# Hybrid encoder block with product-key experts: the last four value tiles by result block, four weight buffers, and norm_final's vector ahead of the root

## What is computed

```python
def peer_ffn(x, ...):           # g: softmax weights of the picked experts, u, v: their rows
    a = gelu(einsum('td,thkd->thk', xb, u))
    return einsum('thk,thkd->td', g * a, expert_v[idx])

h = h + peer_ffn(rmsnorm(h, norm_ffn), ...)
return rmsnorm(h, norm_final)   # y * rsqrt(mean(y*y) + 1e-6) * norm_final
```

## Time and profile before

| | |
|---|---|
| median of 3 runs | 1021.51 us (1021.49 to 1021.79) |
| the profiled execution | 1021.52 us, its span 1019.7 us |
| TensorE matmul busy | 1009.3 us, 99% of the span |
| VectorE, ScalarE, GpSimd busy | 847.5, 599.5, 81.1 us |
| granted TensorE clock, mean | 0.998 |

### The profile page before, as it was taken

The page is one execution under the profiler, slowest core; times in us unless marked ns, Lnnn a source line. Parts: engine busy times, 40 slices in busy tenths (PEclk is TensorE's granted clock), DMA queues, the critical chain, the costliest instruction groups (busy, mean ns, idle before and its releaser), DMA issues.

```text
span 1019.7 us, 20585 instructions
## 1 busy us (share of the span) xinstructions
PE 1009.3 (99%) x6978; PEld 929.4 (91%) x6978; DVE 847.5 (83%) x1686; ACT 599.5 (59%) x1109; POOL 81.1 (8%) x38
## 2 busy tenths in 40 slices
PE   9999999999999999999999999999999999999997
PEld 8989899999999999999999999988888888888885
DVE  7886868679999999999999999777777777777775
ACT  6456544644545468888888888555554544445453
POOL 0000000067780000000000000000000000000000
PEclk9999999999999999999999999999999999999999
DMA  8534334645577766666566665886676676666761
GB/s 332 189 132 143 126 139 168 201 170 207 172 234 230 237 220 209 208 209 206 199 218 208 209 206 198 274 319 232 232 233 233 232 239 235 234 231 238 234 232 67
DMA packets 86597, 215.00 MB, mean 211 GB/s; under 512 B 9600, under 2 KB 42752, under 8 KB 86016
## 3 DMA queue, kind: packets, MB, share of 16 engines
q1 hardware_dynamic: 86240, 213.53, 61.9%
q10 hardware_dynamic: 288, 0.53, 0.1%
HBM read 195.15 MB, written 18.87 MB: 210 GB/s over the span
## 4 chain that ended last, share of the span: by engine, by line
PE 95%; DVE 3%; ACT 1%; issue 1%; DMA 0%; DVEq 0%; ACTq 0%
PE pO L1087 34%; PE pO L1336 18%; PE pTT L1361 18%; PE pM L1361 17%; PE pSS L1310 1%; PE pTT L1310 1%; PE pSS L1157 1%; PE pM L1194 1%; PE pSS L1279 1%; DVE wlos L666 1%; DVE gates L689 0%; DMA raw<-in_stream 0%; PE pTT L1176 0%; DVE biasm L828 0%; PE pM L1188 0%
## 5 line engine op out<-in xcount | busy, mean ns | idle before, releaser
L456 ACT ACTIVATE whis<-raw 128x1024 fp32r<-128x1024 f32 x328 | 344.6, 1051 | 46.6 <-PE pO L1087 34.6
L666 DVE TENSOR_TENSOR wlos<-raw,whis 128x1024 fp32r<-128x1024 f32 x170 | 206.3, 1217 | 21.2 <-ACT whis L456 20.8
L1087 PE MATMUL pO<-xhi,whis 128*128 128x256 f32 x760 | 214.9, 283 | 0.7 <-DVE wlos L666 0.7
L1087 PE MATMUL pO<-xlo,whis 128*128 128x256 f32 x760 | 212.3, 279 | 0.0
L1087 PE MATMUL pO<-xhi,wlos 128*128 128x256 f32 x760 | 212.1, 279 | 0.0
L1003 DVE TENSOR_TENSOR wlos<-raw,whis 128x1024 fp32r<-128x1024 f32 x125 | 153.2, 1226 | 64.1 <-ACT whis L456 64.0
L616 ACT ACTIVATE ghi<-wfull 128x256 fp32r<-128x256 f32 x128 | 53.5, 418 | 171.8 <-PE pM L1361 171.8
L1087 PEld LDWEIGHTS pO<-xhi,whis 128*128 128x128 f32 x760 | 142.7, 188 | 2.0 <-DVE wlos L666 1.6
L1336 PE MATMUL pO<-xlo,whis 128*128 128x256 f32 x512 | 143.4, 280 | 0.0
L1336 PE MATMUL pO<-xhi,wlos 128*128 128x256 f32 x512 | 143.0, 279 | 0.0
L1336 PE MATMUL pO<-xhi,whis 128*128 128x256 f32 x512 | 143.0, 279 | 0.0
(11 more groups left out here) (215 smaller groups left out, 1882.7 us busy)
## 6 DMA issues: line engine op xcount, KB each, us to landing
raw<-in_stream SPq DMA_DIRECT2D x200, 512.0 KB, 3.6
raw<-in_vrows SPq DMA_DIRECT2D x128, 512.0 KB, 3.5
a_scratch<-ast SPq DMA_DIRECT2D x128, 128.0 KB, 1.8
aring<-a_scratch SPq DMA_DIRECT2D x128, 128.0 KB, 3.2
biasm<-in_bias SPq DMA_DIRECT2D x1, 2048.0 KB, 9.6
keysT<-in_keys SPq DMA_DIRECT2D x1, 1024.0 KB, 8.0
h_scratch<-h1tok SPq DMA_DIRECT2D x1, 1024.0 KB, 6.4
htok<-h_scratch SPq DMA_DIRECT2D x1, 1024.0 KB, 8.6
```

Of the source, the lines that this page charges most:

```text
L456: act.activation(whi[s], raw[s][:], ACT.Copy).then_inc(hi_ready, 1)
L666: dve.tensor_tensor(wlo[t % RING], raw[t % RING][:], whi[t % RING].bitcast(F32), ALU.subtract).then_inc(lo_ready, 1)
L1087: last = pe.matmul(dst, st, mv, start=(c == 0 and q == 0), stop=(c == len(terms) - 1 and q == 2))
```

## The change

The last four value tiles are taken out of the tile order. TensorE goes over five pieces of the result, and for each over the four tiles 124 to 127 and their three terms, twelve matmuls. The pieces are three blocks of 512 columns and, for the last 512 columns of the second token block, two of 256. The last two pieces are summed in the banks pO, free by then, and what tiles 0 to 123 have summed in acc[1][1] is added to htok beforehand. For that the high and low weights ghi and glo get four buffers each instead of two, and ghi waits for the tile four back. The loop's first tile moves from 4 to 3.

In the tail the first token block is treated as before. In the second, each piece is multiplied with norm_final before the root is known (gained), by an operation of its own, and afterwards only with the reciprocal: columns 0 to 767 on VectorE, stored by SP, and columns 768 to 1023 on ScalarE, stored by ScalarE's queue. The sum of the first two pieces is scaled by 1/1024 on VectorE and enters the root as its bias. Squares are written to a PSUM bank in place of the SBUF tile fsq.

```diff
+PIECES = ((0, 0, 512), (0, 512, 1024), (1, 0, 512), (1, 512, 768), (1, 768, 1024))
+BY_DVE = 768
...
+        ends = [pT[0], pT[1], pM[0][:], pO[0][:, 0:T], pO[1][:, 0:T]]
...
-                    act.wait_ge(tile_done, i + (T_V - 1))
-                act.activation(ghi[s % 2][:], wfull[s % 2][:], ACT.Copy).then_inc(ghi_ready, 1)
+                    act.wait_ge(tile_done, i + (T_V - RING + 1))
+                act.activation(ghi[s % RING][:], wfull[s % 2][:], ACT.Copy).then_inc(ghi_ready, 1)
...
+            piece_sum(0)
+            piece_sum(1)
+            act.wait_ge(fin_ms, 1)
+            act.activation(fin[:, 6:7], fin[:, 5:6], ACT.Sqrt, scale=1.0 / D).then_inc(fin_root, 1)
+            piece_sum(2)
+            piece_sum(3)
+            piece_sum(4)
+            act.wait_ge(fin_sum, 5)
+            act.wait_ge(fin_ms, 2)
+            act.activation(fin[:, 9:10], fin[:, 4:5], ACT.Sqrt, scale=1.0 / D, bias=fin[:, 8:9]).then_inc(fin_root, 1)
+            act.wait_ge(fin_inverse, 2)
+            act.wait_ge(gained_out, 3)
+            act.activation(htok[:, 1, BY_DVE:D], htok[:, 1, BY_DVE:D], ACT.Copy, scale=fin[:, 10:11]).then_inc(act_rows, 1)
+            act.wait_ge(act_rows, 1)
+            act.dma_start(out[:, 1, BY_DVE:D], htok[:, 1, BY_DVE:D]).then_inc(out_stored, 16)
...
-                dve.tensor_tensor(glo[s % 2][:], wfull[s % 2][:], ghi[s % 2][:].bitcast(F32), ALU.subtract).then_inc(glo_ready, 1)
+                dve.tensor_tensor(glo[s % RING][:], wfull[s % 2][:], ghi[s % RING][:].bitcast(F32), ALU.subtract).then_inc(glo_ready, 1)
...
+            def gained(j):
+
+                b, lo, hi = PIECES[j]
+                dve.wait_ge(fin_sum, j + 1)
+                dve.tensor_tensor(htok[:, b, lo:hi], htok[:, b, lo:hi], gf[:, lo:hi], ALU.mult).then_inc(gained_out, 1)
...
+            dve.wait_ge(tile_done, T_V + NE_TILES - RING)
+            link(dve.tensor_tensor(htok[:, 1, 512:D], acc[1][1], htok[:, 1, 512:D], ALU.add))
             residual(0)
             residual(1)
+            dve.wait_ge(fin_sum, 2)
+            dve.scalar_tensor_tensor(fin[:, 5:6], fin[:, 0:1], D * EPS, fin[:, 1:2], ALU.add, ALU.add).then_inc(fin_ms, 1)
+            dve.wait_ge(fin_root, 1)
+            dve.reciprocal(fin[:, 7:8], fin[:, 6:7]).then_inc(fin_inverse, 1)
+            dve.wait_ge(fin_inverse, 1)
+            rows_out(0)
             residual(2)
-            whole_sum(0)
+            rows_out(1)
             residual(3)
...
+            gained(2)
+            gained(3)
+            dve.wait_ge(fin_sum, 4)
+            link(dve.scalar_tensor_tensor(fin[:, 11:12], fin[:, 2:3], D * EPS, fin[:, 3:4], ALU.add, ALU.add))
+            dve.tensor_scalar(fin[:, 8:9], fin[:, 11:12], 1.0 / D, None, ALU.mult).then_inc(fin_ms, 1)
+            residual(4)
+            gained(4)
+            dve.wait_ge(fin_root, 2)
+            dve.reciprocal(fin[:, 10:11], fin[:, 9:10]).then_inc(fin_inverse, 1)
+            dve.wait_ge(fin_inverse, 2)
+            dve.wait_ge(gained_out, 3)
+            dve.tensor_scalar(htok[:, 1, 0:BY_DVE], htok[:, 1, 0:BY_DVE], fin[:, 10:11], None, ALU.mult).then_inc(out_ready, 1)
...
+            def v_last_tiles():
+
+                for j, (b, lo, hi) in enumerate(PIECES):
+                    last = None
+                    for s in range(RING):
+                        if (b, lo) == (0, 0):
+                            v_wait(NE_TILES - RING + s)
+                        for n, (st, mv) in v_terms(s, b):
+                            last = pe.matmul(ends[j], st, mv[:, lo:hi], start=hi - lo < 512 and s == 0 and n == 0, stop=s == RING - 1 and n == 2)
+                    last.then_inc(acc_done, 1)
```

More of the change, by code:

```diff
@@ L222, in build @@
         G = sbs(top, "G", [P, T, NK])
-        fin = sbs(top, "fin", [P, 10])
+        fin = sbs(top, "fin", [P, 12])
         iota = sbs(top, "iota", [P, P])[:]
@@ L235, in build @@
             gf = sbs(vphase, "gf", [P, D])
-            fsq = sbs(vphase, "fsq", [P, D])
-            glo = [sbs(vphase, f"glo{s}", [P, T], F32R) for s in range(2)]
+            ghi_more = [sbs(vphase, f"ghi{s}", [P, T], F32R) for s in range(2, RING)]
+            glo_more = [sbs(vphase, f"glo{s}", [P, T], F32R) for s in range(2, RING)]
+            glo = [sbs(vphase, f"glo{s}", [P, T], F32R) for s in range(2)] + glo_more
             vpad = sbs(vphase, "vpad", [P, 2, T])
@@ L240, in build @@
             wfull = [sbs(vphase, f"wfull{s}", [P, T]) for s in range(2)]
-            ghi = [sbs(vphase, f"ghi{s}", [P, T], F32R) for s in range(2)]
+            ghi = [sbs(vphase, f"ghi{s}", [P, T], F32R) for s in range(2)] + ghi_more
         def K(name):
@@ L332, in build @@
         h2_ready = sem("h2_ready")
+        gained_out = sem("gained_out")
         fin_sum = sem("fin_sum")
@@ L335, in build @@
         fin_root = sem("fin_root")
+        fin_inverse = sem("fin_inverse")
+        act_rows = sem("act_rows")
         out_ready = sem("out_ready")
@@ L428, in _ @@
                     load_a(g * RAW + s, s)
-            for j in range(2 * TB):
+            for j, at in enumerate(((0, slice(0, 512)), (0, slice(512, D)), (1, slice(0, BY_DVE)))):
                 sp.wait_ge(out_ready, j + 1)
-                half = (slice(None), j // 2, slice((j % 2) * 512, (j % 2 + 1) * 512))
-                sp.dma_start(out[half], htok[half]).then_inc(out_stored, 16)
-            sp.wait_ge(out_stored, 16 * 2 * TB)
+                sp.dma_start(out[:, at[0], at[1]], htok[:, at[0], at[1]]).then_inc(out_stored, 16)
+            sp.wait_ge(out_stored, 16 * 4)
         @block.gpsimd
@@ L1045, in residual @@
             def residual(j):
-                b, q = j // 2, j % 2
+                b, lo, hi = PIECES[j]
                 dve.wait_ge(acc_done, j + 1)
[L1048 to L1065, removed]
+                dve.tensor_tensor(htok[:, b, lo:hi], ends[j], htok[:, b, lo:hi], ALU.add).then_inc(h2_ready, 1)
@@ new lines, in gained, with rows_out @@
+            def gained(j):
+                b, lo, hi = PIECES[j]
+                dve.wait_ge(fin_sum, j + 1)
+                dve.tensor_tensor(htok[:, b, lo:hi], htok[:, b, lo:hi], gf[:, lo:hi], ALU.mult).then_inc(gained_out, 1)
+            def rows_out(q):
+                part = htok[:, 0, q * 512:(q + 1) * 512]
+                dve.scalar_tensor_tensor(part, part, fin[:, 7:8], gf[:, q * 512:(q + 1) * 512], ALU.mult, ALU.mult).then_inc(out_ready, 1)
+            dve.wait_ge(tile_done, T_V + NE_TILES - RING)
@@ L1347, in _, with v_terms, v_wait, v_tile @@
             pe.wait_ge(gbanks_free, 2 + G_STEPS)
-            def v_tile(i, s, first=False, final=False):
+            def v_terms(s, b):
+                vh = whi[s].rearrange("p c n -> p (c n)")
+                vl = wlo[s].rearrange("p c n -> p (c n)")
+                wh, wl = ghi[s][:, b * P:(b + 1) * P], glo[s][:, b * P:(b + 1) * P]
+                return enumerate(((wh, vh), (wh, vl), (wl, vh)))
+            def v_wait(i):
                 pe.wait_ge(lo_ready, i + (T_V + 1))
                 pe.wait_ge(glo_ready, i + 1)
-                vh = whi[s].rearrange("p c n -> p (c n)")
-                vl = wlo[s].rearrange("p c n -> p (c n)")
+            def v_tile(i, s, first=False, closed=None):
+                v_wait(i)
@@ L1354, in v_tile @@
                 last = None
                 for b in range(TB):
[L1356 to L1363, removed]
@@ L1364, in v_tile @@
-                if not final:
-                    last.then_inc(tile_done, 1)
-            for s in range(RING):
+                    for n, (st, mv) in v_terms(s, b):
+                        for q in range(2):
+                            last = pe.matmul(acc[b][q], st, mv[:, q * 512:(q + 1) * 512], start=first and n == 0, stop=n == 2 and (b, q) == closed)
+                last.then_inc(tile_done, 1)
+            def v_last_tiles():
[4 more added lines that the diff above has]
+                            v_wait(NE_TILES - RING + s)
+                        for n, (st, mv) in v_terms(s, b):
+                            last = pe.matmul(ends[j], st, mv[:, lo:hi], start=hi - lo < 512 and s == 0 and n == 0, stop=s == RING - 1 and n == 2)
+                    last.then_inc(acc_done, 1)
@@ L1368, in _ @@
+            for s in range(RING - 1):
                 v_tile(s, s, first=s == 0)
             with pe.Fori(0, (NE_TILES - 2 * RING) // UNROLL) as g:
[L1370 to L1373, removed]
+                for n in range(RING - 1, RING - 1 + UNROLL):
+                    v_tile(g * UNROLL + n, n % RING)
+            v_tile(NE_TILES - RING - 1, RING - 1, closed=(1, 1))
@@ L1376, in constants @@
+            v_last_tiles()
 def constants():
```

18 lines of the change are left out of this document (4 added, 14 removed).

## The result

| | kernel before | changed kernel |
|---|---|---|
| median of 13 executions each | 1021.62 us | 1024.36 us (1022.46 to 1024.54) |
| ratio, 95% interval | | 1.0022 (1.0014 to 1.0029) |
| profiled execution, its span | 1021.52, 1019.7 us | 1022.62, 1020.4 us |

The change costs time. Its executions fall into two groups: of 35 in three comparisons, 17 took 1022.46 to 1023.24 us and 18 took 1024.14 to 1024.76 us, none between. Those of the kernel before stay within 0.7 us in each of the three. So the ratio is one of a mixture. In the first comparison eight of 13 were long ones. In all 35 the two groups differ in the same two records: the short ones have a span of 1020.3 to 1021.1 us and a mean granted clock of 0.998 or 0.999, the long ones a span of 1022.0 to 1022.5 us and a clock of 0.997. What lies outside the span is alike, 2.13 to 2.26 us. The profiled execution is a short one.

A forecast was written before the change was run, and what follows sets the result against it. TensorE, without gaps, was taken to bound the value stage, leaving only the end open. TensorE's end +2.15, tail -1.67 and last stores +0.62 gave +1.1: span 1020.8 plus 1.82 outside, 1022.6 us; stated range 1021.2 to 1024.0.

The forecast's parts named there:

- The stall: First of the last pieces: TensorE waits for glo of tile 126, costing 2.13 us (1.95 to 2.6), about 1.85 us idle.
- Four buffers: Value stage: ghi no longer waits for TensorE two tiles back; by itself this gives nothing.
- The tail up to the last compute: From TensorE's end to the last compute: 4.11 us becomes 2.44, a gain of 1.67.
- The 768 columns: Last multiplication on VectorE, by the reciprocal: 0.56 us taken, 0.92 as the slow alternative.
- The end of the span and what lies outside: Last compute to end of span: 2.72 becomes 3.34 us; outside the span 1.82 us, as before.
- The clock: TensorE after the stall: granted clock stays full until TensorE is done, so no time is lost to it.
- rival (a): Stall also drops TensorE's clock: 4 us at half speed, 2 us lost, 1024.6 us; chance 0.13.
- VectorE has no idle time between 1012.2 and 1016: Sign for the changed kernel's trace, in the tail: VectorE continuously busy over that stretch.
- the forecast's own range: Whole kernel: 1022.1 to 1023.4 us, from stall 1.95 to 2.6 and last transfer -0.3 to +0.5.
- slower by over 0.2%: Outcome case for the whole kernel, above 1023.55 us: rival (a) and half of (c), chance 0.19.
- Rival (b): Tiles 126 and 127 are ready thanks to four buffers, TensorE ends at 1012.87, time 1020.5 us; chance 0.07.
- (c): Tail gives nothing: ScalarE's transfer or VectorE's waits on itself cost 0.9 us more, time 1023.5 us; chance 0.12.

The follow-up runs named there:

- e4: Kernel before with four buffers of ghi and glo, ghi's wait moved to the tile four back, squares in a PSUM bank: 1021.53 us, ratio 0.9999.
- e3: Changed kernel with three tiles by result block in place of four: 1022.15 us, ratio 1.0005.
- e7: Changed kernel with two tiles by result block in place of four: 1023.38 us, ratio 1.0016.
- e8: Changed kernel with only the last tile by result block, so the new tail and four buffers by themselves: 1024.74 us, ratio 1.0030.
- e9: e4 plus its last three tiles by result block of 512 columns, keeping the tail of before: 1021.52 us, ratio 1.0000.
- e1: Changed kernel with eight unread matmuls of 512 columns filling TensorE's stall: 1022.86 us, ratio 1.0012.
- e5: Changed kernel unaltered, executed again: 1023.00 us, four of 11 executions long, the profiled one short.
- e10: Changed kernel with three tiles by result block, first half multiplied with norm_final by piece and scaled on ScalarE, gained(3) behind residual(4): 1020.89 us, ratio 0.9993.
- e11: Changed kernel unaltered, executed once more: 1024.14 us, six of 11 executions long, the profiled one long at 1024.53.
- e2: Changed kernel with two more additions of 512 columns on VectorE ahead of tile 127's product weights, lengthening the stall: 1025.65 us, ratio 1.0042.
- e6: Changed kernel with four unread matmuls filling half of TensorE's stall: 1023.42 us (1022.76 to 1024.32).
- e12: The kernel of e6 executed once more: 1023.22 us (1022.76 to 1023.95).

## Why the prediction was right and where it was wrong

- **The stall** was right in size and place. Predicted were 1.85 us of idle, released by glo of tile 126; measured 1.90. whi of tile 127 was to start 0.20 after the first piece (1001.70 against 1001.50); 0.26. From first to last matmul of the pieces 13.24 predicted, 13.27 measured, so also the restart and the 256-column matmuls (24 of them from 1011.98 to 1014.60, one every 0.114 us, predicted 0.117) hold.
- **Four buffers cost and give nothing**: e4 shows it.
- **The tail up to the last compute**: predicted 2.44, measured 2.42. The gap for residual(4) behind VectorE's queue is there (ready 1014.88, taken 1015.15), and e3, e7 and e8 show how it grows when the pieces come closer. The 768 columns took 0.62; I had 0.56 and, as the other end, 0.92. At 0.6 ns a column above 0.16 us it is nearer to the rate of L966 (0.53) than to that of L796 (0.98). The Trainium skill's VectorE: DVE Perf Modes (The perf-mode tier table) has tensor_scalar on float32 in SBUF at twice the plain rate, and this row agrees.
- **The end of the span and what lies outside** were two errors that cancelled. Last compute to end of span: 3.34 predicted, 3.10 measured, as the last bytes flowed at up to 430 GB/s. Outside the span I took the 1.82 us of before; the changed kernel has 2.22. Nothing in my steps provided for that, and what causes it is open. The sum, 1022.6, met the profiled 1022.62 partly by luck.
- **The clock** is the step that failed: the forecast put it at nothing. I gave rival (a) 0.13, with the argument that 1.85 us of idle are fewer than the 2.5 after which the clock fell at the end of the span. But after 1.90 us of idle the clock fell in the long execution that was profiled, and 18 of 35 have its span and its mean clock. They set the median, 1024.36, beyond my upper bound of 1024.0 and 0.24 below the 1024.6 of that rival. A row in which the clock falls after 2.5 us only says that 2.5 are enough; it says nothing for 1.9, and I read it as a threshold. The price was near: 4 us at half speed and 2.0 lost were assumed, 3.4 us and 1.53 lost measured. The Trainium skill's TensorE: Matmul & The Clock Gate (HAM oscillation) warns that matmuls which wait for their operands come back at half the clock. The long execution agrees (granted clock 0.50 in the windows behind the gap), the short one with the same gap doesn't (1.00).
- **The signs.** "VectorE has no idle time between 1012.2 and 1016" did not hold: it stood 0.57 us, up to 1016.14, for the last sum. The prediction's own steps had this pause (residual(4) to 1015.78, gained(4) from 1016.35), so the sign contradicted them. And the forecast's own range adds up to 1023.6 at its upper end, not 1023.4: 1022.6 with 0.47 for the stall and 0.5 for the last transfer. The short group, 1022.46 to 1023.24, lies inside either.
- By the chances, "slower by over 0.2%" had 0.19, and it is where the ratio of 1.0022 lies, though its interval (from 1.0014) reaches into the neighbouring case.
- Rival (b) is refuted by the gap itself, and (c) by the 5.5 us from TensorE's end to the end of the span (1014.88 to 1020.4), 0.3 less than I had.

## What to carry to other kernels

Working by result block brings the first results forward, but asks for all operands of the block at its start: write down when the last operand can be ready at the pace of the ring it lives in, and take as many tiles as just fit (three here, where four stall). A pause of TensorE has to be priced twice, once for its length and once for the clock behind it, and for the second a distribution of executions is needed, since one profile shows one side of it. Compare spans as well as times: they tell a slower kernel from time that lies outside the span. And a tail moved under matmuls is worth only what the in-order queue of its busiest engine lets through before the last piece.

## What was not expected of the hardware

- The same pause, in the same kernel, left the granted clock at 2.4 GHz in two profiled executions (1.90 and 1.89 us) and was followed by 3.4 us at 1.2 GHz in a third (1.90 us). After a pause of 3.35 us the clock was down in the one seen, and all four executions have the time and the mean clock that go with it. With pauses of 0.96 and 0.97 us it was full in the two seen, and the 21 spans show no loss.
- With the pause filled by matmuls whose result nobody reads, the long executions were gone, at no cost (median 1022.86 us, that of the short group 1022.90).
- The time outside the span differs by kernel: 1.74 to 1.87 us in the executions of the kernels that store by SP alone (before, e4, e9), 2.13 to 2.29 in those of the changed kernel and of most that end with a store from ScalarE's queue (e1, e3, e5, e7, e8, e10, e11). e2, which also does, had 1.75 to 1.86, and e6 and e12, which differ from e1 only in the number of filling matmuls, 2.14 to 3.43. So that the queue is the cause was not shown, and neither was the cause of that spread.
